# An expert stage with 96 token slots, and one turn in seven moved from TensorE to VectorE

## The reference, cut to what matters

```python
def swiglu(h, w_gate_up, w_down):
    g, u = jnp.split(h @ w_gate_up, 2, axis=-1)
    return (jax.nn.silu(g) * u) @ w_down

def moe_ffn(h, router, w_gate_up, w_down):
    ...
    top_v, top_i = lax.top_k(logits, TOP_K)          # 2 of 8 experts for each of the 256 tokens
    gates = jax.nn.softmax(top_v, axis=-1)
    ...
    for e in range(N_EXPERTS):
        out = out + combine[:, e:e + 1].astype(t.dtype) * swiglu(t, w_gate_up[e], w_down[e])
```

## Time and profile before

| | |
|---|---|
| time, median of 3 runs | 1419.13 us (1418.8 to 1419.32) |
| the profiled execution, from first to last instruction | 1417.7 us |
| PE busy | 1411.1 us (100%) |
| DVE busy | 1234.8 us (87%) |
| ACT busy | 964.5 us (68%) |
| POOL busy | 101.9 us (7%) |
| granted TensorE clock over the span | 1.000 |
| expert stage | from about 469 us to the end |

### The profile page before, as it was taken

How to read it: one execution, slowest core, us unless ns; L and a number is a source line. 1 busy time by engine, 2 the same in 40 slices (tenths; PEclk the granted TensorE clock), 3 DMA queues, 4 the chain that set the end, 5 groups by cost and what they waited for, 6 DMA issues and landing times.

```text
span 1417.7 us, 19898 instructions
## 1 busy us (share of the span) xinstructions
PE 1411.1 (100%) x6721; PEld 1185.2 (84%) x6721; DVE 1234.8 (87%) x1207; ACT 964.5 (68%) x840; POOL 101.9 (7%) x147
## 2 busy tenths in 40 slices
PE   9999999999999999999999999999999999999999
PEld 8998888888988888888888888888888888888887
DVE  6486888878677898999989999999999999999887
ACT  7465544443694677777777777787777777777775
POOL 4010000000022020010010000001001000000000
PEclk9999999999999999999999999999999999999999
DMA  9554655564445799999999999999999999999995
GB/s 321 163 180 147 219 196 178 178 204 144 127 177 194 274 384 389 375 378 393 379 382 394 374 374 396 394 374 382 393 371 382 395 382 374 395 383 382 383 393 195
DMA packets 212592, 442.93 MB, mean 312 GB/s; under 512 B 16372, under 2 KB 56760, under 8 KB 212544
## 3 DMA queue, kind: packets, MB, share of 16 engines
q1 hardware_dynamic: 208640, 430.18, 83.0%
q0 software_dynamic: 3888, 12.13, 2.9%
q10 hardware_dynamic: 16, 0.00, 0.0%
HBM read 434.88 MB, written 7.37 MB: 312 GB/s over the span
## 4 chain that ended last, share of the span: by engine, by line
PE 98%; ACT 1%; DVE 1%; issue 0%; POOL 0%; ACTq 0%; DVEq 0%; POOLq 0%
PE PS L1729 21%; PE PS L1730 21%; PE PS L1733 21%; PE PS L1431 5%; PE PS L1430 5%; PE PS L1432 5%; PE PS L1162 3%; PE PS L1218 2%; PE PS L1210 2%; PE PS L1212 2%; PE PS L1269 1%; PE PS L1275 1%; PE PS L1272 1%; PE PS L1718 1%; PE PS L1192 1%; PE PS L1721 1%
## 5 line engine op out<-in xcount | busy, mean ns | idle before, releaser
L1884 DVE TENSOR_TENSOR wlo<-ring,whi 128x2048 fp32r<-128x2048 f32 x334 | 758.8, 2290 | 53.3 <-ACT whi L799 51.2
L799 ACT ACTIVATE whi<-ring 128x2048 fp32r<-128x2048 f32 x334 | 639.8, 1918 | 184.3 <-PE PS L1733 173.8
L1729 PE MATMUL PS<-whi,xhi 128*128 128x512 f32 x864 | 340.8, 394 | 0.0
L1730 PE MATMUL PS<-whi,xlo 128*128 128x512 f32 x864 | 336.6, 390 | 0.0
L1733 PE MATMUL PS<-wlo,xhi 128*128 128x512 f32 x864 | 231.0, 389 | 0.0
L1733 PEld LDWEIGHTS PS<-wlo,xhi 128*128 128x128 f32 x864 | 162.1, 188 | 34.0 <-DVE wlo L1884 0.2
L1730 PEld LDWEIGHTS PS<-whi,xlo 128*128 128x128 f32 x864 | 162.4, 188 | 32.4
L1729 PEld LDWEIGHTS PS<-whi,xhi 128*128 128x128 f32 x864 | 162.3, 188 | 32.4
L1729 PE MATMUL PS<-whi,hhi 128*128 128x512 f32 x440 | 171.4, 389 | 0.0
L1730 PE MATMUL PS<-whi,hlo 128*128 128x512 f32 x440 | 171.2, 389 | 0.0
L1733 PE MATMUL PS<-wlo,hhi 128*128 128x512 f32 x440 | 117.8, 390 | 0.0
(11 more groups left out here) (387 smaller groups left out, 1637.1 us busy)
## 6 DMA issues: line engine op xcount, KB each, us to landing
ring<-in_moe_w_gate_up SPq DMA_DIRECT2D x448, 512.0 KB, 6.7
ring<-in_moe_w_down SPq DMA_DIRECT2D x224, 512.0 KB, 7.2
ring<-in_dense_w_gate_up SPq DMA_DIRECT2D x56, 512.0 KB, 4.6
ring<-in_dense_w_down SPq DMA_DIRECT2D x28, 512.0 KB, 4.1
ring<-in_a_w_in SPq DMA_DIRECT2D x12, 768.0 KB, 8.6
ring<-in_mem_w_kv SPq DMA_DIRECT2D x4, 1024.0 KB, 7.7
ring<-in_a_w_out SPq DMA_DIRECT2D x4, 1024.0 KB, 5.3
ring<-in_b_w_out SPq DMA_DIRECT2D x4, 1024.0 KB, 7.3
```

Source lines behind the costliest of these rows:

```text
L799: nc.scalar.activation(whi[:, j, :], ring[:, h * SLOT:(h + 1) * SLOT], ACT.Copy).then_inc(S("highs"), 1)
L1729: mm(out_, lhsT=xh, rhs=whi[:, j, c0:c0 + HD], start=begin, stop=False)
L1730: mm(out_, lhsT=xl, rhs=whi[:, j, c0:c0 + HD], start=False, stop=False)
L1884: v.tensor_tensor(wlo[:, j, :], ring[:, h * SLOT:(h + 1) * SLOT], whi[:, j, :].bitcast(F32), ALU.subtract).then_inc(S("lows"), 1)
```

## The change

`CAP` goes from 128 to 96. The operands that TensorE holds stay 128 wide: it reads 128 columns of `xhi`, `xlo`, `hhiE` and `hloE`, of which the last 32 belong to no slot (or to the next chunk), and the results in partitions 96 to 127 of PSUM are not read. What works on the slots themselves gets narrower: the turned hidden rows (128x384 instead of 128x512), the token rows (128x768 instead of 128x1024), the indirect transfers (96 rows instead of 128). `turn_rows` has 12 pieces instead of 16. The number of possible passes goes from 2 to 3, which adds one chained VectorE operation to the count and two to `gates`.

For block 0 of the later experts TensorE no longer transposes. VectorE does, in 12 pieces of 32x128: six after the low part of cut (1, 0), six after that of cut (1, 1).

```diff
-CAP = 128
+CAP = 96
+        hTE = carve(4096, 4, CAP)
-        xe_ = slice(0, CAP)
+        xe_, wide_ = slice(0, CAP), slice(0, P)
+        hhiW, hloW = ([bass.AP(h.tensor, h.offset + c * CAP, [list(h.ap[0]), [1, P]]) for c in range(4)] for h in (hhiE, hloE))
+        def vector_turns(i, b):
+
+            return b == 0 and not is_first(i)
...
-            def hidden_high(n):
+            def hidden_high(n, by_vector=False):
 
                 act.wait_ge(S("h_turned"), n)
-                nc.scalar.activation(hhiE, PS[:, 3, 0:4 * CAP].rearrange("p (c s) -> p c s", c=4), ACT.Copy).then_inc(S("h_high"), 1)
+                nc.scalar.activation(hhiE, hTE if by_vector else PS[:, 3, 0:4 * CAP].rearrange("p (c s) -> p c s", c=4), ACT.Copy).then_inc(S("h_high"), 1)
...
-            def turn_expert(n):
+            def turn_expert(n, by_vector=False):
 
                 pe.wait_ge(S("h_ready"), n)
+                if by_vector:
+                    return
                 for c in range(4):
                     last = tr(PS[:, 3, c * CAP:(c + 1) * CAP], hnE[:, c * P:(c + 1) * P])
                 last.then_inc(S("h_turned"), 1)
...
+            def turn_hidden(n, squares):
+
+                dve.wait_ge(S("h_ready"), n)
+                for k in squares:
+                    r, q = divmod(k, 4)
+                    done = v.transpose(hTE[32 * q:32 * q + 32, :, 32 * r:32 * r + 32],
+                                       hnE[32 * r:32 * r + 32].rearrange("p (c q f) -> p c q f", c=4, q=4)[:, :, q, :])
+                if k == CAP // 8 - 1:
+                    done.then_inc(S("h_turned"), 1)
...
                     if b < NBE - 1:
                         if b > 0 or not first:
                             expert_lo(i, b + 1, 0)
+                        if vector_turns(i, b):
+                            turn_hidden(i * NBE + (NB + b + 1), range(CAP // 16))
                         expert_lo(i, b + 1, 1)
+                        if vector_turns(i, b):
+                            turn_hidden(i * NBE + (NB + b + 1), range(CAP // 16, CAP // 8))
                     if 1 < b < 6 and not first and not last:
                         if b == 2:
                             dve.wait_ge(S("rows_in"), i * 16 + 16)
-                        turn_rows(range(4 * (b - 2), 4 * (b - 1)))
+                        turn_rows(range(CAP // 32 * (b - 2), CAP // 32 * (b - 1)))
```

More of the change, by code:

```diff
@@ L59, in build @@
     PASSES = -(-SEQ // CAP)
-    assert CAP <= P
+    assert CAP <= P and CAP % 32 == 0
     x_d, mem_d = T["x"][0], T["mem"][0]
@@ L292, in build @@
         o = 2 * NT * FB
-        Sx = carve(o, NT, CAP); o += NT * CAP
+        Sx = carve(o, NT, P); o += NT * P
         tok_f = carve(o, NT); o += NT
         gate, gate_next = carve(o, 1)[0:CAP], carve(o + 1, 1)[0:CAP]; o += 2
-        xe_ = slice(0, CAP)
+        xe_, wide_ = slice(0, CAP), slice(0, P)
+        hhiW, hloW = ([bass.AP(h.tensor, h.offset + c * CAP, [list(h.ap[0]), [1, P]]) for c in range(4)] for h in (hhiE, hloE))
         NC = PASSES * NE
-        iota = carve(o, CAP); o += CAP
-        iotai = arena[:, o:o + CAP].bitcast(I32); o += CAP
+        iota = carve(o, P); o += P
+        iotai = arena[:, o:o + P].bitcast(I32); o += P
         m8 = carve(o, NT, 8); o += NT * 8
@@ L305, in build @@
         picked = carve(o, NT + 1, NE); o += (NT + 1) * NE
-        first_slot = carve(o, CAP); o += CAP
+        first_slot = carve(o, P); o += P
         key = carve(o, NT); o += NT
@@ L310, in build @@
         place_at = carve(o, 3, 2 * NT); o += 6 * NT
+        over_at = carve(o, 2 * NT); o += 2 * NT
         place_i = arena[:, o:o + 2 * NT].bitcast(I32); o += 2 * NT
@@ L663, in _ @@
             pool.wait_ge(S("att_out"), 1)
-            pool.iota(iotai, pattern=[[1, CAP]], base=0, channel_multiplier=0).then_inc(S("iota"), 1)
+            pool.iota(iotai, pattern=[[1, P]], base=0, channel_multiplier=0).then_inc(S("iota"), 1)
             pool.wait_ge(S("iota"), 1)
@@ L672, in _ @@
             pool.memset(blank[:, :, 0], 0.0).then_inc(S("iota"), 1)
-            pool.tensor_copy(blank[:, :, 1], iota[0:NC + 1]).then_inc(S("iota"), 1)
-            pool.tensor_scalar(blank[:, :, 2], iota[0:NC + 1], float(SEQ), None, ALU.add).then_inc(S("iota"), 1)
+            pool.tensor_copy(blank[:, :, 1], iota[0:NC + 1, 0:CAP]).then_inc(S("iota"), 1)
+            pool.tensor_scalar(blank[:, :, 2], iota[0:NC + 1, 0:CAP], float(SEQ), None, ALU.add).then_inc(S("iota"), 1)
             pool.wait_ge(S("iota"), 8)
@@ L813, in expert @@
                         expert_hi(i, b, 2)
-                        hidden_high(i * NBE + (NB + b))
+                        hidden_high(i * NBE + (NB + b), by_vector=b > 0 and vector_turns(i, b - 1))
                     if b == 1 and not first:
@@ L1688, in gather @@
                 for k in ks:
-                    last = mm(PS[:, 6 + k // KH, (k % KH) * CAP:(k % KH + 1) * CAP], lhsT=xn[:, t, k * P:(k + 1) * P], rhs=Sx[:, t, :],
+                    last = mm(PS[:, 6 + k // KH, (k % KH) * CAP:(k % KH + 1) * CAP], lhsT=xn[:, t, k * P:(k + 1) * P], rhs=Sx[:, t, 0:CAP],
                               start=(t == 0 and k % KH == 0), stop=(t == NT - 1), skip_group_check=True)
@@ L1742, in expert_gate_up @@
                     expert_cut(i, b, q, j, [
-                        (PS[0:CAP, expert_bank(i, b) + g, :], xhi[:, 2 * q + kk, xe_], xlo[:, 2 * q + kk, xe_], kk * D + g * EB, q == 0 and kk == 0,
+                        (PS[:, expert_bank(i, b) + g, :], xhi[:, 2 * q + kk, wide_], xlo[:, 2 * q + kk, wide_], kk * D + g * EB, q == 0 and kk == 0,
                          q == 3 and kk == 1) for kk in range(2) for g in range(2)])
@@ L1787, in expert @@
                     if b > 0 or not first:
-                        turn_expert(i * NBE + (NB + b + 1))
+                        turn_expert(i * NBE + (NB + b + 1), by_vector=vector_turns(i, b))
             expert(0)
@@ L1800, in _ @@
                         c, c0 = 2 * (q - 4) + kk, kk * D + hh * HD
-                        y_last = three(PS[0:CAP, 4 + hh, :], xhi[:, c, xe_], xlo[:, c, xe_], whi[:, j, c0:c0 + HD], wlo[:, j, c0:c0 + HD],
+                        y_last = three(PS[:, 4 + hh, :], xhi[:, c, wide_], xlo[:, c, wide_], whi[:, j, c0:c0 + HD], wlo[:, j, c0:c0 + HD],
                                        False, c == 3)
@@ L1904, in gates @@
                 then(v.tensor_tensor(place_at[:, 2], place_at[:, 0], place_at[:, 1], ALU.add))
+                for q in range(2, PASSES):
+                    then(v.tensor_scalar(over_at, place_at[:, 0], float(q * CAP), float((NE - 1) * CAP), ALU.is_ge, ALU.mult))
+                    then(v.tensor_tensor(place_at[:, 2], place_at[:, 2], over_at, ALU.add))
                 then(v.scalar_tensor_tensor(out=place_at[:, 1].rearrange("p (c t) -> p c t", c=2), in0=bass.AP(idxf.tensor, idxf.offset, ends[:1] + [[1, 2], [NE, NT]]),
@@ L1929, in next_dispatch @@
                     for t in range(NT):
-                        part = v.tensor_scalar(Sx[:, t], iota, put_at[:, t:t + 1], None, ALU.is_equal)
+                        part = v.tensor_scalar(Sx[0:CAP, t], iota[0:CAP], put_at[:, t:t + 1], None, ALU.is_equal)
                     part.then_inc(S("dispatch"), 1)
@@ L1942, in turn_rows @@
                 for n in squares:
-                    (r, c), last = divmod(n, 4), n == 15
-                    done = v.transpose(xsT[32 * c:32 * c + 32].rearrange("p k (q s) -> p k q s", q=4)[:, :, r, :],
+                    (r, c), last = divmod(n, 4), n == CAP // 8 - 1
+                    done = v.transpose(xsT[32 * c:32 * c + 32].rearrange("p k (q s) -> p k q s", s=32)[:, :, r, :],
                                        xs[32 * r:32 * r + 32].rearrange("p (k q f) -> p k q f", k=KD, q=4)[:, :, c, :])
@@ L1969, in expert @@
                         expert_lo(i, b, 2)
-                        hidden_low(i * NBE + (NB + b))
+                        hidden_low(i * NBE + (NB + b), by_vector=b > 0 and vector_turns(i, b - 1))
                     expert_lo(i, b, 3)
```

8 lines of the change are left out of this document (4 added, 4 removed).

## The result

The changed kernel takes 1428.85 us (median of 4 runs, 1428.14 to 1429.14), the kernel before on the same chip 1419.22 us. The ratio is 1.0068, with a 95% interval from 1.0056 to 1.0081: slower by 9.6 us. The forecast was 1425.8 us. The measured time lies in the range that was to hold 8 in 10 (1419.5 to 1429.5) and 0.35 us above the forecast's own range (1423.0 to 1428.5).

What follows compares the result with a forecast made beforehand. TensorE sets the pace, VectorE close behind. On the profiled span of 1417.7 us, +6.7 + 0.5 - 0.5 = +6.7 gives 1424.4; the median lies 1.4 us higher: 1425.8 us, own range 1423.0 to 1428.5, 8 in 10 1419.5 to 1429.5.

Steps and rivals of the forecast that it cites:

- The mechanism: Block 1 of seven later experts: work queued behind VectorE's squares makes each expert 0.95 us longer, +6.7 us.
- the rival with squares at 0.20 us: Squares cheap enough that TensorE's saved turns stand: 1415.3 us, down to 1413.9; chance 9%.
- That ScalarE's queue does the harm: Block 1: hidden_high waits 3.5 us for squares and stands ahead of the high part of (1, 3) that TensorE wants soon.
- TensorE's wait: Cuts (1, 2) and (1, 3) of later experts: about 1.45 us in two or three pieces.
- a sign: Profile after: PE idle 1.2 to 1.7 us together in cuts (1, 2) and (1, 3) of each of seven experts.
- The matmuls on the weights keep their shape and their 2.72 us a cut: nothing there: Expert stage: TensorE's matmul cuts, 2.72 us each, were to stay unchanged with 96 slots, at no cost.
- The narrow turns: Six turns per expert left on TensorE, streaming 96 columns instead of 128: gain 0.5 us, bounds 0 and 1.9.
- The late scatter: VectorE's next_dispatch waits for a later scatter, delaying the low part of (2, 0): 0.5 us taken, 0 to 4.2 possible.
- The period of an expert: Time from one later expert to the next: from 117.5 to 118.4 us.
- TensorE's clock: Rival: the granted clock falls behind TensorE's new waits, costing half the speed while it lasts; chance 1%.

Runs made afterwards that it cites:

- e6_act_order: The change with ScalarE's y_out and high part of (1, 3) put ahead of hidden_high in block 1 of later experts; 1424.46 us (1.0038).
- e4_vector_turn_128: The change with CAP back at 128, so block 0 is turned by VectorE in 16 squares; 1442.6 us (1.0168).
- e12_before_lo_shifted: The kernel before with hlo alone begun 128 bytes later, hhi left in place; 1427.83 us (1.0062).
- e9_order_1443: The change with chunks 512 bytes apart, hidden_high behind the high part of (1, 3), squares spread one, four, four, three, token rows turned a block later; 1413.65 us (0.9958).

## Why the prediction was right, and by what

**The mechanism: right, its price near.** The squares were to cost 6.7 us; taken alone, on the change's own chunks, they cost 6.2 (1428.85 - 1422.69). The two numbers have different baselines: the 6.7 are against turns of 128 columns, the 6.2 against turns of 96, which for seven experts are some 0.6 us cheaper, so 5.6 us compare with 6.7. On chunks 512 bytes apart, as the forecast had them, it is 8.0 us, or 7.4, with 0.6 us of the wait for rows in it. Step by step from the low part of (1, 0): second low part at +4.09 us (forecast +4.19), squares over and `hidden_high` at +8.33 (+8.48), `y_out` at +8.76 (+8.95), the high part of (1, 3) at +9.76 (+9.95), its low part at +11.69 (+11.90). The squares came in at 0.315 us each, and 0.30 long; the rival with squares at 0.20 us fell with that. The 194 ns estimated from the Trainium skill's formula ("VectorE: DVE Perf Modes", section "The TRN2 errata") are too low here: the measurement is 302.

**That ScalarE's queue does the harm: right**, by `e6_act_order`, for two thirds of it.

**TensorE's wait: 1.12 us, not 1.45**, under the 1.2 to 1.7 us that I had named as a sign. The chain was 0.2 us shorter, and TensorE reached block 1 later than I took it to, because its down cuts were slow. From the low part of (1, 0) on VectorE to TensorE's matmuls on that of (1, 3) it is 847.28 - 833.24 = 14.04 us, against 844.52 - 831.27 = 13.25 before: +0.79, forecast +0.95. A term that the forecast did not have, the restart behind the last wait, adds 0.13 us (2.89 against 2.76). So two errors of about 0.15 us cancel in each expert, and that part of the agreement is luck.

**"The matmuls on the weights keep their shape and their 2.72 us a cut: nothing there" failed.** Shape is not all: chunks at 384 bytes made 110 down cuts some 0.07 us longer each, 7.8 us with the turns on TensorE. This is the large miss, and nothing in my text would have found it: the diff showed the new start of the held operand, and I read no row that tests one.

**The narrow turns were mis-sized.** I took 0.5 us with a bound of 1.9; they gain 4.4 over 55 turns, 3.8 over the 48 that this term was for. Four transposes of 96 columns take 0.27 us of the path (819.34 to 819.61 in the change), where four of 128 take 0.36, in proportion to the columns. The rows that I leaned on held narrower operands but streamed 128 columns, or were 4x4 and four in number, with an end that the model rounds.

**The late scatter: nothing.** `next_dispatch` went on at 852.15, 9.05 us after `y_out`'s end, with no wait in any expert; 0.5 us were taken.

The two unforeseen sizes cancel in part: against the forecast of +6.7 us, the squares came to +6.2, the chunks to +7.8, the narrow turns to -4.4, which is +9.6. The overlap of 2 us is in it, as the squares are taken on slow chunks and the chunks without squares. The forecast of 1425.8 us is near the result because one term put at nothing cost 7.8 us and another gained 3.9 us more than it was given: that is luck. The period of an expert shows it, 960.87 - 842.00 = 118.87 us from one `y_out` to the next, where I had named 118.4.

**TensorE's clock: right for the change**, where it was 1.00 throughout. That the rival was no empty one shows in `e4_vector_turn_128`.

## What to carry to other kernels

When work moves to an engine that is second in line, ask what stands behind the operation that waits for it on a third engine: there the order of two instructions was worth some 4.3 of 6.2 us, and could be mended without touching the work itself. When a tile gets narrower, keep where its parts start: look at the start addresses of held operands in a diff, not only at the shapes. And when the bounding engine is busy without a gap, price an edit by the time from one start to the next, and count a new wait as somewhat longer than it is.

## What the runs showed of the hardware that I had not expected

- With the float32 operands that TensorE holds (`hhi`, `hlo`) begun 128 bytes later in their tiles, a matmul takes about 0.233 us from start to start instead of 0.227, 10.6 us in all; begun 256 bytes later they cost nothing (1419.25 us).
- A badly placed held operand slows its own matmul and the one just ahead, not the one behind (397, 396 and 391 ns in the dense layer of `e12_before_lo_shifted`, 389 or 390 before). With one held operand in three shifted this gives 9.05 of the 10.6 us.
- Held operands of 96 columns are slower than of 128: 0.230 against 0.227 us a matmul, 10.1 us.
- A matmul group that waited even 0.03 us (2.75 us in `e9_order_1443` where 2.72 is undisturbed) is followed by a cut about 0.15 us longer (2.85 to 2.88 against 2.72 us). The granted clock stayed at 1.00, the level of 2.4 GHz, over these stretches.
- After an idle time of 1.73 us the granted clock fell to 0.50, the level of 1.2 GHz, in two of seven experts of `e4_vector_turn_128`, for 3.4 us each, at a price of 1.1 us each.
